# Scores of block 1 as three products of rounded parts, and modulation sums in two buffers

## What is computed

```python
# block 1, stick-breaking head: z are the scores
z = jnp.einsum('bhqd,bhkd->bhqk', q_blk, k).astype(jnp.float32) * scale
log_beta = jax.nn.log_sigmoid(z)
log_1mb = jnp.where(strict, jax.nn.log_sigmoid(-z), 0.0)
...
# block 1, differential head: two maps of scores, m = 0, 1
logits = jnp.einsum('bhmqd,bhmkd->bhmqk', q_blk, k).astype(jnp.float32) * scale
...
# block 2
mod = c @ w_ada[l] + b_ada[l]
shift_m, scale_m, gate_m, shift_f, scale_f, gate_f = jnp.split(mod, 6, axis=-1)
```

## Time and profile before

| what | value |
|---|---|
| median of 3 runs | 2822.47 us (2819.86 to 2824.04) |
| profiled execution, its own time | 2822.24 us |
| its span, first to last instruction | 2820.4 us |
| PE busy | 2723.1 us (97% of the span) |
| DVE busy | 1648.4 us (58%) |
| POOL busy | 1596.2 us (57%) |
| ACT busy | 859.5 us (30%) |
| mean granted clock of PE | 0.993 |

### The profile page before, as it was taken

How to read it: one execution, slowest core, us unless ns; L and a number is a source line. 1 busy time by engine, 2 the same in 40 slices (tenths; PEclk the granted TensorE clock), 3 DMA queues, 4 the chain that set the end, 5 groups by cost and what they waited for, 6 DMA issues and landing times.

```text
span 2820.4 us, 38224 instructions
## 1 busy us (share of the span) xinstructions
PE 2723.1 (97%) x13138; PEld 2180.2 (77%) x13138; DVE 1648.4 (58%) x2348; ACT 859.5 (30%) x1696; POOL 1596.2 (57%) x1242
## 2 busy tenths in 40 slices
PE   7999999899999999999999999989999999999998
PEld 5677777676878888887788887767787878888887
DVE  5666687738467777777734303484445446556556
ACT  4555445535312112114422114554233100100102
POOL 3555511455987777765523243222366987777764
PEclk9999999999999999999999999999999999999999
DMA  3322321034111111124411342213424021111134
GB/s 137 102 89 83 94 94 53 16 137 153 57 45 60 53 45 59 52 82 160 179 45 45 89 145 98 74 61 108 159 97 157 31 68 45 59 52 45 59 126 143
DMA packets 76777, 243.75 MB, mean 86 GB/s; under 512 B 7119, under 2 KB 10992, under 8 KB 76276
## 3 DMA queue, kind: packets, MB, share of 16 engines
q1 hardware_dynamic: 54576, 184.31, 20.0%
q10 hardware_dynamic: 22084, 57.86, 5.8%
HBM read 207.00 MB, written 32.52 MB: 85 GB/s over the span
## 4 chain that ended last, share of the span: by engine, by line
PE 81%; DVE 8%; POOL 5%; ACT 3%; issue 2%; DMA 0%; POOLq 0%; ACTq 0%; DVEq 0%
PE ps L817 16%; PE ps L819 16%; PE ps L818 16%; PE ps L1129 7%; PE ps L1130 7%; PE ps L1131 7%; PE ps L901 2%; PE ps L917 2%; POOL arena L707 1%; PE ps L1412 1%; PE ps L1424 1%; PE ps L932 1%; DVE ps L2492 1%; DVE ps L2509 1%; DVE ps L2533 1%
## 5 line engine op out<-in xcount | busy, mean ns | idle before, releaser
L640 POOL CAST wh<-raw 128x1024 fp32r<-128x1024 f32 x175 | 187.3, 1070 | 842.0 <-PE ps L819 799.0
L817 PE MATMUL ps<-hh,wh 128*128 128x512 f32 x1456 | 598.4, 411 | 8.1 <-DVE hl L2453 3.6
L819 PE MATMUL ps<-hh,wl 128*128 128x512 f32 x1456 | 571.1, 392 | 0.0
L818 PE MATMUL ps<-hl,wh 128*128 128x512 f32 x1456 | 569.9, 391 | 0.0
L642 POOL TENSOR_TENSOR wl<-raw,wh 128x1024 fp32r<-128x1024 f32 x175 | 421.9, 2411 | 14.0
L733 POOL TENSOR_TENSOR wl<-raw,wh 128x512 fp32r<-128x512 f32 x256 | 344.3, 1345 | 20.5
L817 PEld LDWEIGHTS ps<-hh,wh 128*128 128x128 f32 x1456 | 275.6, 189 | 79.1 <-issue 20.7
L819 PEld LDWEIGHTS ps<-hh,wl 128*128 128x128 f32 x1456 | 274.4, 188 | 59.9
L818 PEld LDWEIGHTS ps<-hl,wh 128*128 128x128 f32 x1456 | 275.7, 189 | 52.5 <-issue 3.4
L817 PE MATMUL ps<-gated,wh 128*128 128x512 f32 (+1 forms) x728 | 279.7, 384 | 3.5 <-DVE gated L2543 3.2
L818 PE MATMUL ps<-gated,wh 128*128 128x512 f32 (+1 forms) x728 | 278.4, 382 | 0.0
(11 more groups left out here) (341 smaller groups left out, 5080.5 us busy)
## 6 DMA issues: line engine op xcount, KB each, us to landing
raw<-weights SPq DMA_DIRECT2D x271, 512.0 KB, 3.5
arena<-w_ada SPq DMA_DIRECT2D x48, 512.0 KB, 3.8
arena<-gate_scratch ACTq DMA_DIRECT2D x20, 512.0 KB, 5.2
arena<-x_t ACTq DMA_DIRECT2D x1, 4096.0 KB, 14.2
x_scratch<-arena ACTq DMA_DIRECT2D x2, 2048.0 KB, 8.4
arena<-x_scratch SPq DMA_DIRECT2D x2, 2048.0 KB, 10.2
gate_scratch<-arena ACTq DMA_DIRECT2D x16, 256.0 KB, 2.2
x_scratch<-arena ACTq DMA_DIRECT2D x1, 4096.0 KB, 13.6
```

What stands on the lines that cost most here:

```text
L640: pool.tensor_copy(wh[:, s], raw[:, r]).then_inc(Z.wt_hi, 1)
L817: pe.matmul(out, wh[:, slot, w], xh, start=start, stop=False)
L818: pe.matmul(out, wh[:, slot, w], xl, start=False, stop=False)
L819: return pe.matmul(out, wl[:, slot, w], xh, start=False, stop=stop)
```

## The change

The scores become three fp32r products. ACT now rounds q and k into fp32r tiles `Q_HI` and `K_HI`, DVE subtracts them from PSUM into low parts (`low_out`, `fill_low_out`), and `a_scores` adds high x high, high q x low k, and low q x high k in PSUM, the two sides in turn. A piece of scores has at least 256 columns. PE's fills of q and k wait for the low parts (`f_low`) where they waited for ACT's copies (`f_ev`). The low parts of q of even jobs lie where modulation sums lay, so the sums now use two buffers in turn: `mod_add(s)` runs in step s (it was `mod_add(s - 1)`), `modulation(g)` and `mod_out(g)` stand at step 8 + 8g (it was 10 + 8g), and at step 32 they come ahead of the other work. The block of scratch for descriptors is 512 bytes in place of 1024.

```diff
-        Q_T, K_T = [T(0), T(2)], [T(1), T(3)]
+        Q_HI, K_HI = [qk[:, 0], qk[:, 2]], [qk[:, 1], qk[:, 3]]
+        K_LO = [low3[:, 0], low3[:, 1]]
+        def q_lo(i):
+            return low3[:, 2] if i % 2 else low_a[:, {0: 0, 2: 1, 4: 3, 6: 5}[i]]
...
-        MOD_IN, MOD_ACC = T(13), [T(14), T(12), T(14), T(12), T(14), T(24)]
+        MOD_IN, MOD_ACC = T(13), [T(12), T(14), T(12), T(14), T(14), T(24)]
...
-        MOD_AT = {10 + 8 * g: g for g in range(6)}
+        MOD_AT = {8 + 8 * g: g for g in range(6)}
...
                     if k == 0 and n >= 2:
-                        pe.wait_ge(Z.f_ev, fill_evicted(n - 2))
+                        if (n - 2) % 6 < 4:
+                            pe.wait_ge(Z.f_low, fill_low(n - 2))
+                        else:
+                            pe.wait_ge(Z.f_ev, fill_evicted(n - 2))
...
+                parts = ((Q_HI[i % 2], K_HI[i % 2]), (Q_HI[i % 2], K_LO[i % 2]), (q_lo(i), K_HI[i % 2]))
                 for c in range(0, w, HALF):
-                    e = min(w, c + HALF)
-                    for side in range(2):
-                        r = slice(DH * side, DH * (side + 1))
-                        last = pe.matmul(bank(2 * side, 2)[:, c:e], Q_T[i % 2][r, query(s)], K_T[i % 2][r, c:e],
-                                         start=True, stop=True, skip_group_check=True)
+                    e = max(min(w, c + HALF), c + 2 * P)
+                    for n, (q, k) in enumerate(parts):
+                        for side in range(2):
+                            r = slice(DH * side, DH * (side + 1))
+                            last = pe.matmul(bank(2 * side, 2)[:, c:e], q[r, query(s)], k[r, c:e],
+                                             start=(n == 0), stop=(n == 2), skip_group_check=True)
...
+                if s == SB_N:
+                    modulation(MOD_AT[s])
...
-                if s in MOD_AT:
+                if s in MOD_AT and s != SB_N:
                     modulation(MOD_AT[s])
...
+            def low_out(hi, lo, ps, scale):
+                if scale == 1.0:
+                    dve.tensor_tensor(lo, ps, hi.bitcast(F32), ALU.subtract).then_inc(Z.f_low, 1)
+                else:
+                    dve.scalar_tensor_tensor(lo, ps, scale, hi.bitcast(F32), ALU.mult, ALU.subtract).then_inc(Z.f_low, 1)
+            def fill_low_out(n):
+                i, kind, t = 1 + n // 6, n // 2 % 3, half_of(n % 2)
+                dve.wait_ge(Z.f_ev, fill_evicted(n))
+                if n == 6:
+                    dve.wait_ge(Z.e_out, 64)
+                hi, lo = ((Q_HI[i % 2], q_lo(i)), (K_HI[i % 2], K_LO[i % 2]))[kind]
+                low_out(hi[:, t], lo[:, t], bank(6 + n % 2), 1.0 if kind else DH ** -0.5)
...
+            for n, (hi, lo) in enumerate(((Q_HI[0], q_lo(0)), (K_HI[0], K_LO[0]))):
+                dve.wait_ge(Z.f_ev, n + 1)
+                low_out(hi, lo, bank(2 * n, 2), 1.0 if n else DH ** -0.5)
...
-                if 1 <= s <= 48:
-                    mod_add(s - 1)
+                if s < 48:
+                    mod_add(s)
...
+                for n in fills_done(s):
+                    if n % 6 < 4:
+                        fill_low_out(n)
```

More of the change, by code:

```diff
@@ L157, in build @@
         reset = place("reset", [P, S])
+        low3 = place("low3", [P, 3, S], F32R)
+        qk = place("qk", [P, 4, S], F32R, ARENA_AT)
+        low_a = place("low_a", [P, 6, S], F32R, ARENA_AT + 4 * 9 * S)
         ps = ctx.enter_context(nc.psum_tensor("ps", [P, 8 * HALF], F32))
@@ L181, in build @@
         n_sq n_sum n_ss n_ln n_rstd n_t n_hi n_lo f_ln f_rstd f_y f_x
-        f_half f_ev t_full t_free z_full pv_full o_ev
+        f_half f_ev f_low t_full t_free z_full pv_full o_ev
         mask_in s_mask s_reset s_u s_b s_c s_a d_near d_max d_nmx d_exp d_r d_m d_w
@@ L288, in build @@
             if _s in TURN_AT:
+                if _s == SB_N:
+                    T_AT["mod", MOD_AT[_s]] = turns
+                    turns += 1
                 for _side, _lo, _hi in turned(TURN_AT[_s]):
@@ L292, in build @@
             for _kind, _table in (("v", V_AT), ("e", E_AT), ("mod", MOD_AT), ("ss", SS_AT)):
-                if _s in _table:
+                if _s in _table and (_kind, _s) != ("mod", SB_N):
                     T_AT[_kind, _table[_s]] = turns
@@ L575, in _ @@
             for s in range(FILL_STEPS):
[L576 to L581, removed]
+                for g in ((0, 1) if s == 0 else (s + 1,)):
+                    if g < 48:
+                        if g == 0:
+                            sp.wait_ge(Z.n_lo, 16)
+                        else:
+                            sp.wait_ge(Z.mod_acc, g)
+                        sp.dma_start(MOD_IN, A.w_ada[g % 8, :, (g // 8) * 1024:(g // 8 + 1) * 1024]).then_inc(Z.mod_in, 16)
                 for n in range(6, C_WO + SL):
@@ L895, in a_scores @@
                 if s % NB == 0:
-                    pe.wait_ge(Z.f_ev, fill_evicted(6 * (i - 1) + 3) if i else 2)
+                    pe.wait_ge(Z.f_low, fill_low(6 * (i - 1) + 3) if i else 2)
+                parts = ((Q_HI[i % 2], K_HI[i % 2]), (Q_HI[i % 2], K_LO[i % 2]), (q_lo(i), K_HI[i % 2]))
                 for c in range(0, w, HALF):
-                    e = min(w, c + HALF)
-                    for side in range(2):
-                        r = slice(DH * side, DH * (side + 1))
-                        last = pe.matmul(bank(2 * side, 2)[:, c:e], Q_T[i % 2][r, query(s)], K_T[i % 2][r, c:e],
-                                         start=True, stop=True, skip_group_check=True)
-                        if e == w:
-                            last.then_inc(Z.z_full, 1)
+                    e = max(min(w, c + HALF), c + 2 * P)
[4 more added lines that the diff above has]
+                                             start=(n == 0), stop=(n == 2), skip_group_check=True)
+                            if n == 2 and e >= w:
+                                last.then_inc(Z.z_full, 1)
             def a_turn(s, side, lo, hi):
@@ L1731, in _ @@
             act.preload_act_table_set("sigmoid_and_others")
-            for n, dst in enumerate((Q_T[0], K_T[0], HVT)):
+            for n, dst in enumerate((Q_HI[0], K_HI[0], HVT)):
                 act.wait_ge(Z.chunk_done, C_QKV + n + 1)
@@ L2592, in mod_add @@
                 if k == 0:
+                    if g == 4:
+                        dve.wait_ge(Z.t_full, T_AT["mod", g - 1] + 1)
+                    elif g == 5:
+                        dve.wait_ge(Z.pv_full, SB_N)
                     dve.tensor_scalar(MOD_ACC[g], MOD_IN, col("c", k), None, ALU.mult).then_inc(Z.mod_acc, 1)
```

8 lines of the change are left out of this document (6 added, 2 removed).

## The result

The changed kernel takes 2832.85 us (median; 2832.23 to 2834.92) where the kernel before took 2822.17 beside it. The ratio is 1.0046, with an interval of 1.0036 to 1.0056. The prediction said 2829.0, slower, within 2813.5 to 2838. The sign and the two main terms, the new waits and the clock falls behind them, were right; the clock's term was less than half of what the profiled execution shows.

A forecast was written before the change was run, and what follows sets the result against it. The prediction took PE's own work to bound the kernel. From 2822.24 us it took 9.2 for scores and added 7.9 for waits, 0.7 for subtractions, 1.0 for step 0 and 6.4 for the clock: 2829.0, range 2813.5 to 2838.

The forecast's parts named there:

- scores: Attention scores on PE: three fp32r products, both sides overlapping at the price of full rows, gain 9.2 us over eight jobs.
- waits behind `v_out`: End of steps 8, 16, 24, 40, 48: PE's modulation waits for DVE's copy of `v_turn`, 7.9 us more.
- subtractions ahead of `d_max`: Steps 35, 43, 51: DVE's subtraction delays the next `d_max` and the scores after it, 0.7 us.
- `v_out` in step 0: Step 0: `mod_add(0)` stands ahead of `v_out`, so the copy PE needs comes later, 1.0 us.
- clock, attention stage: A half-clock fall at each of the five new waits, one old fall gone; 6.4 us net, between -1.6 and +9.
- Rivals 3 and 4: Scores: sides don't overlap in fp32r, 2881 us, chance 0.07; weight loads stand on the path, 2853 us, chance 0.03.
- Rival 1: Attention stage: the new waits come but the clock stays up; 2822.6 us, or 2821 without the old fall; chance 0.22.
- Rival 2: Faster scores move DVE's chain, so `v_out` is early enough for the modulation; 2813.3 us, no new waits or falls; chance 0.13.

The follow-up runs named there:

- e8_split: e7_best with the modulations of steps 8, 16, 24, 40 and 48 cut in two halves around one group of fills; 2808.15 us, ratio 0.9957.
- e9_split_f32: e8_split with its scores as one float32 product of the high parts at the old widths; 2817.99 us, ratio 0.9989.
- e2_early: The changed kernel with every modulation directly behind the scores of its step and its sum copied out earlier; 2812.55 us, ratio 0.9973.
- e4_nolow: The changed kernel without DVE's subtractions, all three products taking the high parts; 2832.20 us, ratio 1.0040.
- e7_best: e2_early with DVE's copy of `v_turn` ahead of the first term of the sum in step 0; 2811.81 us, ratio 0.9965.
- e11_again: The changed kernel itself, unaltered, run again; 2831.93 us, ratio 1.0039.
- e3_f32: The changed kernel with its scores as one float32 product of the high parts at the old widths; 2837.92 us, ratio 1.0062.
- e6_128: The changed kernel with scores cut at their true width, pieces of 128 columns where it takes 256; 2829.12 us, run once.
- e1_busy: The changed kernel with PE kept busy in its waits by products whose result nobody reads; 2822.65 us, ratio 1.0008.
- e5_serial: The changed kernel with side 0's three products written ahead of side 1's three, for each piece; 2834.6 us, run once.

## Why the prediction was right, and where it was not

Its sum was +6.8 against the profiled execution; measured were +12.7 (2834.92 less 2822.24).

| term | predicted | measured |
|---|---|---|
| scores | -9.2 | -9.1 |
| waits behind `v_out` | +7.9 | +7.3 |
| subtractions ahead of `d_max` | +0.7 | 0 |
| cover lost in steps 34, 35, 42, 50 | | +1.5 |
| `v_out` in step 0 | +1.0 | +1.4 |
| clock, attention stage | +6.4 | +15.1 |
| later stages | | -2.6 |
| sum | +6.8 | +13.6 |

The later stages are the time from the last scores to the end, 2263.7 and 2261.1 us; there the profile after has two stretches at half the clock fewer. The measured terms overshoot by 0.9; 0.6 of it is that the first scores start that much earlier (57.19 against 57.80), whose cause is open. Against the medians the miss is smaller than in this profile: 2832.85 is 3.9 over the forecast. The sign was no sure call: the prediction itself gave "slower" 0.42 and "same" 0.44.

- **Scores: right.** Three pairs at the price of full rows, both sides beside each other. e8_split against e9_split_f32 gives 9.0 to 9.8, and agrees. Rivals 3 and 4 are out.
- **Waits: right to 0.6.** Steps 8, 16 and 24 cost 1.32 more each, as forecast. Step 40 cost 1.98 (0.27 and 2.45 against 0.74), step 48 1.29: there the 2.71 was 0.7 too long. With the modulation elsewhere these waits are gone but for 0.29 and 0.9 (e2_early).
- **The cost of the subtractions: term and cause wrong.** The 0.7 us for a subtraction that "stands ahead of the next `d_max`" is refuted by the traces: PE's waits near there are the same in e4_nolow, without the subtractions. The time adds no more than that it is the same within the intervals. No wait of PE on the 22 us of DVE's new work shows. What I called a mere move, the modulation that "leaves steps 10, 18, 26, 34, 42, 50", cost 1.5: new waits stand where it left, and what it covered there is, by exclusion, their cause. I had asked what the new place costs, and not what the old place had hidden.
- **Step 0: 0.4 low,** just over the bound of 1.3 (1.4 is step 1 of e2_early less that of e7_best). I did not ask there whether a wait of 3.1 us brings a fall; it did at 70.03, but not in e11_again, where the wait was 2.9.
- **The clock: the term that was mis-sized.** "I take a fall at each of the five" held in both profiles. "1.6 each" did not: I took one stretch of 3.41 for each fall, as in the earlier trace rows, where the falls at 153.39 and 525.40 last one. In the first profile the five falls were nine stretches, and steps 1 and 33 added two falls that no term held. 11 x 3.41 less 0.5 of idle is 37.0, half of it 18.5; less the 3.4 of before it is 15.1. My upper end for this term was 9. With the seven stretches of e11_again it would be 8.5: there the five falls were six stretches, and 1.6 each was nearly right.
- **What the length of a fall goes with** is where it comes in the modulation. The six profiles with a modulation behind `v_turn` and PE idle in the wait (the changed kernel twice, e3_f32 to e6_128) have 30 such falls. In 14 the fall came 1.4 us or more before the modulation's end, so that the one-column products ran at half the clock, and it lasted 6.83 or 10.24. In the other 16 the modulation was over, or had at most 0.33 to go, and it lasted 3.41. The narrow scores behind it made no difference: in step 8 of e11_again and step 40 of the first profile they ran in the slow time too, and it lasted 3.41. The same program has both, so the number of stretches in one profile is in part luck, and the forecast's bound of 9 for this term left it too little room.
- **Rival 1, the clock stays, is refuted** by the rows at 134.88, and e1_busy shows what the clock cost at the least: 10.2 us by the medians, with the waits left in and three stretches still there.
- **Rival 2 did not come as I wrote it,** but its time did. 2813.3 was the price of the change without the new waits and falls, and e2_early, which takes the new waits of the five places and their falls away, ran in 2812.55. That the two are so close is partly luck: e2_early still has the 3.0 us wait of step 1, 0.9 in steps 40 and 48, and three stretches at half the clock.

## What to carry to other kernels

A change that shortens PE's work can lose at a place where a wait is put ahead of thin matmul work: price the wait, then the clock behind it, once with the thin work ahead of the fall and once within the slow time, where it lasted two or three times as long here. A step that moves leaves a hole as well: ask which waits it had covered where it stood. Reducing products of one column can be cut up between wide ones: they took 1.8 us in e8_split and 1.9 whole in e2_early, and no fall stood behind the cut ones in three profiles. That this gains time over the uncut ones is not shown.

## What the runs showed of the chip that I had not expected

- Products on different rows of the array ran in another order than the kernel writes them: in e5_serial one started 0.33 us ahead of a product that precedes it in the kernel (194.868 and 195.20), and serial order cost nothing (1.58 us for 1024 columns in both). The Trainium skill, "TensorE: Matmul & The Clock Gate", Part 3, "The mechanism", has weight loads pulled ahead when the row group differs, which agrees; it also has matmuls start strictly in program order, and here the trace differs, unless the compiled program already had the other order.
- Start to start, fewer columns than 256 gained next to nothing here: 0.12 us for a pair of 256 columns, 0.11 for a pair of 128, 0.11 for a product of one column.
- Busy time does not tell whether the clock holds: in e1_busy it fell at 136.74 behind stretches in which PE was busy for 3.33 of 3.41 and 3.38 of 3.42 us, the last of them with one-column products. The same wait of 1.87 us ahead of step 33 brought a fall in both profiles of the changed kernel and none in the kernel before or in e8_split.
